# GpSimd splits weight slabs in quarters, and the mLSTM head loop is software-pipelined by one head

## The reference

```python
proj = xn @ w_in                                   # 1024 -> 4096
xm, z = jnp.split(proj, 2, axis=-1)                # 4 heads of 512 each
xp = jnp.concatenate([conv_state, xm], axis=1)
xc = conv_b + sum(xp[:, j:j + L] * conv_w[j] for j in range(4))
xc = jax.nn.silu(xc)
q = jnp.einsum('blhd,hde->blhe', xc_by_head, wq)   # and k
v = jnp.einsum('blhd,hde->blhe', xm_by_head, wv)
gates = concat(q, k, v) @ w_gates + b_gates
...
o = jax.nn.sigmoid(z)
```

## Time and profile before

| | before |
|---|---|
| median of three runs | 2535.7 us |
| profiled execution, its own time | 2533.09 us |
| its span | 2531.3 us |
| PE busy | 2311.2 us, 91% |
| PEld busy | 2138.8 us, 84% |
| DVE busy | 1268.1 us, 50% |
| POOL busy | 981.8 us, 39% |
| ACT busy | 340.9 us, 13% |
| mean granted clock of PE | 0.939 |
| chain of waits, by engine | PE 81%, DVE 15%, issue 2%, ACT 2% |

### The profile page before, as it was taken

How to read it: one execution, slowest core, us unless ns; L and a number is a source line. 1 busy time by engine, 2 the same in 40 slices (tenths; PEclk the granted TensorE clock), 3 DMA queues, 4 the chain that set the end, 5 groups by cost and what they waited for, 6 DMA issues and landing times.

```text
span 2531.3 us, 37962 instructions
## 1 busy us (share of the span) xinstructions
PE 2311.2 (91%) x16133; PEld 2138.8 (84%) x16133; DVE 1268.1 (50%) x2092; ACT 340.9 (13%) x578; POOL 981.8 (39%) x309
## 2 busy tenths in 40 slices
PE   7968758899999999989899889999979999999997
PEld 7967657897999999989898766577659889999997
DVE  7765687633635254662653623443444436263354
ACT  4211211212200000120110121220212211000001
POOL 4524553532455555544444420012014244555552
PEclk9988888999999999999999888889889999999998
DMA  5112332310222222224324122241122112222221
GB/s 198 68 67 84 112 105 97 135 66 34 80 78 80 81 83 83 95 93 152 142 103 160 66 72 89 111 160 67 71 86 98 50 51 84 80 78 79 81 83 54
DMA packets 36593, 231.26 MB, mean 91 GB/s; under 512 B 4332, under 2 KB 7404, under 8 KB 10864
## 3 DMA queue, kind: packets, MB, share of 16 engines
q1 hardware_dynamic: 21600, 154.15, 17.2%
q10 hardware_dynamic: 14864, 75.21, 7.6%
HBM read 195.50 MB, written 33.85 MB: 91 GB/s over the span
## 4 chain that ended last, share of the span: by engine, by line
PE 81%; DVE 15%; issue 2%; ACT 2%; DMA 0%; ACTq 0%; DVEq 0%
PE psum L504 63%; PE psum L534 14%; PE psum L520 2%; DVE xnl L1403 2%; DVE xc L1952 1%; DVE bbq L1627 1%; PE psum L530 1%; DVE tm L1603 0%; DVE tm L2124 0%; DVE tm L2123 0%; DVE xnl L2126 0%; DVE x L1774 0%; DVE x L1536 0%; ACT pr L1189 0%; DVE xc L1950 0%
## 5 line engine op out<-in xcount | busy, mean ns | idle before, releaser
L454 POOL TENSOR_SCALAR whi<-raw 128x2048 fp32r<-128x2048 f32 x146 | 289.2, 1981 | 1494.7 <-PE psum L504 1426.4
L504 PE MATMUL psum<-xnh,whi 128*128 128x288 f32 (+1 forms) x2816 | 630.2, 302 | 79.2 <-DVE xnl L1403 30.3
L456 POOL TENSOR_TENSOR wlo<-raw,whi 128x2048 fp32r<-128x2048 f32 x146 | 682.9, 4678 | 12.2
L504 PE MATMUL psum<-xnl,whi 128*128 128x288 f32 (+1 forms) x2816 | 622.9, 300 | 0.0
L504 PE MATMUL psum<-xnh,wlo 128*128 128x288 f32 (+1 forms) x2816 | 622.3, 299 | 0.0
L504 PEld LDWEIGHTS psum<-xnh,whi 128*128 128x128 f32 x2816 | 469.2, 193 | 90.5 <-issue 55.3
L504 PEld LDWEIGHTS psum<-xnl,whi 128*128 128x128 f32 x2816 | 469.1, 193 | 0.0
L504 PEld LDWEIGHTS psum<-xnh,wlo 128*128 128x128 f32 x2816 | 468.9, 193 | 0.0
L504 PE MATMUL psum<-hh,whi 128*128 128x288 f32 x1024 | 220.1, 296 | 0.0
L504 PE MATMUL psum<-hl,whi 128*128 128x288 f32 x1024 | 219.4, 295 | 0.0
L504 PE MATMUL psum<-hh,wlo 128*128 128x288 f32 x1024 | 219.3, 295 | 0.0
(11 more groups left out here) (395 smaller groups left out, 2808.7 us busy)
## 6 DMA issues: line engine op xcount, KB each, us to landing
raw<-in_w SPq DMA_DIRECT2D x146, 1024.0 KB, 4.7
C<-in_C ACTq DMA_DIRECT2D x4, 1024.0 KB, 4.9
o_cp<-mvt ACTq DMA_DIRECT2D x4, 1024.0 KB, 3.9
o_cs<-C ACTq DMA_DIRECT2D x4, 1024.0 KB, 3.9
t_xc<-xc ACTq DMA_DIRECT2D x3, 1152.0 KB, 4.1
t_z<-mv ACTq DMA_DIRECT2D x3, 1152.0 KB, 4.4
t_q<-mq ACTq DMA_DIRECT2D x3, 1152.0 KB, 4.1
t_k<-mk ACTq DMA_DIRECT2D x3, 1152.0 KB, 4.2
```

The source lines that it names most:

```text
L454: pool.tensor_scalar(whi[:, s, :], raw[:, s, :], 1.0, 1.0, ALU.mult, ALU.mult).then_inc(S("slab_hi"), 1)
L456: pool.tensor_tensor(wlo[:, s, :], raw[:, s, :], whi[:, s, :].bitcast(F32), ALU.subtract)\
L504: ins = pe.matmul(bank(g, 2 * m + b)[:, 0:t1 - t0], W[wi][:, kk, m0 + m, :], r[:, kk, t0:t1], start=(at_first and wi == 0 and r is rh), st ...
```

## The change

Three things are changed. First, POOL's `split` works on quarters of 512 columns: four times a tensor_scalar and a tensor_tensor; PE is still told once per slab, after the last. Second, the order of slabs and groups in the mLSTM inputs: xm of the next head comes before q, k, v of this one, z of the next head behind the gate of this one. Third, DVE and ACT follow: DVE does convolution tiles 0 and 1 of the next head before it copies q out, and tiles 2 and 3 each ahead of a z evacuation. For the last head tile 2 stands between the k and v copies. In head 0, tiles 0 and 1 come between the two xm evacuations. ACT does SiLU before it rounds xm, and begins a head's inputs after the stores of the head before.

```diff
@@ schedule(), and the same order in PE's loop
-            for h in range(ML_H):
-                for part in ("xm", "z"):
-                    for i in range(2):
-                        if (h, part, i) != LATE_Z:
-                            s("ml", h, part, i)
-                            g("ml", h, part, i)
+            inputs(0, "xm")
+            inputs(0, "z")
+            for h in range(ML_H):
+                if h + 1 < ML_H:
+                    inputs(h + 1, "xm")
                 for part in ("q", "k", "v"):
                     s("ml", h, part)
                     g("ml", h, part, 0)
                     g("ml", h, part, 1)
                 g("gate", h)
+                if h + 1 < ML_H:
+                    inputs(h + 1, "z")
@@ POOL
-                pool.tensor_scalar(whi[:, s, :], raw[:, s, :], 1.0, 1.0, ALU.mult, ALU.mult).then_inc(S("slab_hi"), 1)
-                pool.wait_ge(S("slab_hi"), i * 2 + (s + 1))
-                pool.tensor_tensor(wlo[:, s, :], raw[:, s, :], whi[:, s, :].bitcast(F32), ALU.subtract)\
-                    .then_inc(S("slab_split"), 1)
+                for piece in range(4):
+                    c = slice(SLAB // 4 * piece, SLAB // 4 * (piece + 1))
+                    pool.tensor_scalar(whi[:, s, c], raw[:, s, c], 1.0, 1.0, ALU.mult, ALU.mult).then_inc(S("slab_hi"), 1)
+                    pool.wait_ge(S("slab_hi"), i * 8 + (4 * s + piece + 1))
+                    ins = pool.tensor_tensor(wlo[:, s, c], raw[:, s, c], whi[:, s, c].bitcast(F32), ALU.subtract)
+                ins.then_inc(S("slab_split"), 1)
@@ ACT
+            head_inputs(0)
+            for h in range(ML_H):
                 if h < ML_H - 1:
                     for w, (nm_, buf) in enumerate((("q", mq), ("k", mk), ("v", mv))):
                         act.wait_ge(S("qkv_ready"), 6 * h + 2 * w + 2)
                         store(A["t_" + nm_][h], buf[:], nm_ + "_spilled")
+                    head_inputs(h + 1)
@@ DVE
+            def conv_inputs(h, i):
+                if h and i == 0:
+                    v.wait_ge(S("xm_hi"), h)
+                    v.wait_ge(S("xm_split"), h)
...
+            def conv(h, t):
+                if h and t == 0:
                     v.wait_ge(S("xc_spilled"), 16 * h)
...
+            for i in range(2):
+                conv_inputs(0, i)
+                conv(0, 2 * i)
+                conv(0, 2 * i + 1)
+            for t in range(ML_T):
+                low_xc(0, t)
+            scale_z(0, 0)
+            low_xm(0)
+            scale_z(0, 1)
+            for h in range(ML_H):
+                nxt = h + 1 < ML_H
+                if nxt:
+                    conv_inputs(h + 1, 0)
+                    conv(h + 1, 0)
+                    conv_inputs(h + 1, 1)
+                    conv(h + 1, 1)
                 for w, (part, buf) in enumerate((("q", mq), ("k", mk), ("v", mv))):
...
+                        if h + 1 == LATE_Z[0] and w == 1 and i == 1:
+                            conv(h + 1, 2)
+                    if nxt and w == 2:
+                        low_xc(h + 1, 0)
+                        low_xc(h + 1, 1)
                 g = GR["gate", h]
...
+                if nxt and h + 1 != LATE_Z[0]:
+                    conv(h + 1, 2)
+                    scale_z(h + 1, 0)
+                    conv(h + 1, 3)
+                    scale_z(h + 1, 1)
+                elif nxt:
+                    conv(h + 1, 3)
+                    scale_z(h + 1, 0)
+                if nxt:
+                    low_xc(h + 1, 2)
+                    low_xc(h + 1, 3)
+                    low_xm(h + 1)
```

More of the change, by code:

```diff
@@ L804, in _, with inputs @@
             mlp(0)
-            for h in range(ML_H):
[L806 to L811, removed]
+            def inputs(h, part):
+                for i in range(2):
+                    if (h, part, i) == (0, "xm", 0):
+                        project_first(3, GR["ml", h, part, i], SL["ml", h, part, i])
+                    elif (h, part, i) != LATE_Z:
+                        project(GR["ml", h, part, i], SL["ml", h, part, i], xnh, xnl)
+            inputs(0, "xm")
+            inputs(0, "z")
+            for h in range(ML_H):
+                if h + 1 < ML_H:
+                    inputs(h + 1, "xm")
                 for w, part in enumerate(("q", "k", "v")):
@@ L1912, in _ @@
             v.memset(xm[:, :, 0:3], 0.0)
[L1913 to L1938, removed]
@@ new lines, in conv_inputs @@
+            def conv_inputs(h, i):
+                if h and i == 0:
+                    v.wait_ge(S("xm_hi"), h)
+                    v.wait_ge(S("xm_split"), h)
+                g = GR["ml", h, "xm", i]
+                group_ready(v, g)
+                for m in range(2):
+                    for b, w, c0, c1, t0 in SEG:
+                        ins = tt(xm[:, 2 * i + m, c1:c1 + w], bank(g, 2 * m + b)[:, c0:c0 + w], rs[:, t0:t0 + w], MUL)
+                ch.mark(ins, free[g % 2], S("xm_ready"))
+                a = PCOL["conv_cache"][0] + 12 * h + 6 * i
+                cc = par[:, a:a + 6].rearrange("p (t k) -> p t k", k=3)
+                two, out = slice(2 * i, 2 * i + 2), slice(4 * h + 2 * i, 4 * h + 2 * i + 2)
+                ch.mark(v.tensor_copy(xm[:, two, TP + 3:TP + 6], cc))
+                v.tensor_copy(cst[:, 0, out, :], xm[:, two, TP:TP + 3])
+                v.tensor_copy(cst[:, 1, out, :], xm[:, two, T + 3:T + 6])
@@ L1958, in _ @@
-                low_xc(ML_T - 1)
-                if h:
-                    v.wait_ge(S("v_spilled"), 16 * h)
-                scale_z(0)
+                for tap in range(4):
+                    for d0, s0, w in ((0, 0, TP), (TP, TP + 3, TS)):
+                        src, dst = xm[:, t, s0 + tap:s0 + tap + w], xc[:, t, d0:d0 + w]
+                        wc = col("conv_w", 16 * h + 4 * t + tap)
+                        if tap == 0:
+                            ins = ts(dst, src, wc, col("conv_b", 4 * h + t), MUL, ADD)
+                        else:
+                            ins = stt(dst, src, wc, dst, MUL, ADD)
+                        ch.mark(ins)
+                    ch.sync()
@@ new lines, in conv, with low_xc, scale_z @@
+                v.sem_inc(S("conv_done"), 1)
+            def low_xc(h, t):
+                v.wait_ge(S("xc_hi"), 4 * h + t + 1)
+                tt(xcl[:, t, :], xc[:, t, :], xch[:, t, :].bitcast(F32), SUB).then_inc(S("xc_split"), 1)
+            def scale_z(h, i):
+                g = GR["ml", h, "z", i]
+                group_ready(v, g)
+                if h and i == 0:
+                    v.wait_ge(S("v_spilled"), 16 * h)
+                for b in range(4):
+                    dst = sz if (h, "z", i) == LATE_Z else mv
+                    ins = tt(halves(dst, 2 * i + b // 2)[b % 2], bank(g, b)[:, 0:HALF], RS[b % 2], MUL)
+                ch.mark(ins, free[g % 2], S("z_scaled"))
@@ L1962, in _, with low_xm @@
+            def low_xm(h):
                 v.wait_ge(S("xm_hi"), h + 1)
```

46 lines of the change are left out of this document (19 added, 27 removed).

## The result

The changed kernel takes 2463.9 us (median of 4 runs, 2461.6 to 2467.0) against 2536.5 us: ratio 0.972, 95% interval 0.970 to 0.973. It gains 72.6 us, where 35 were forecast; 2464 lies 13 us under the low end of the range. Its profiled execution has a span of 2460.2 us (2461.9 us of time), 71.1 less than before. Two executions, one of the kernel before (2913 us) and one of the changed kernel (5610 us), were slow ones and are left out of every comparison and median here.

A forecast was written before the change was run, and what follows sets the result against it. PE was taken as the bound, busy 91% of the span with 81% of the chain of waits. Terms 38.0 + 10 + 2 - 7 - 6 - 3 = 34.0 us gave 2499.1, plus 2.6 for the median: 2501 us, range 2486 to 2514.

The forecast's parts named there:

- The stage, 38.0: mLSTM inputs: projecting the next head's inputs ahead removes PE's holes before q; gain 38.0 us, bounds 33 and 43.
- the 5.9 us: mLSTM inputs: part of the 43.9 us excess that stays: 2.5 + 1.7 head 0, 0.8 heads 1 to 3, 0.9 head 3.
- The norm starts, +10: Starts of the four projections behind a norm: DVE's xnl tiles no longer held 4.3 us; +2.5 us each, +10 us.
- MLP hidden tile 3, -7: Last hidden tile of each MLP quarter, eight times: POOL's later end delays PE; -7 us, bounds 0 and -13.
- 720.6 becomes 721.5: MLP: POOL ends 1.2 us later, only DVE's casts slip in between, so PE's tile starts later by these times.
- POOL late in the MLP: Rival: hand-overs make each of 64 MLP slabs 0.85 us late, 54 us; time 2552 us; chance 0.05.
- S5, -6: S5's dense DVE rows delay slab splitting: -3.5 net including a smaller GLU stall, -2.5 for bbq products; bounds +6 and -12.
- a dense row of them now gives way eight times per slab: DVE rows without pause: quarters make them yield to POOL eight times per slab instead of twice, charged as a loss.
- The first 160 us, -3: Start of the kernel, chains of 0.2 us DVE instructions: -0.5 to -1 us per slab over four slabs, -3 us.
- Lone stalls, +2: Smaller stalls of lone DVE instructions on the chain: +2 us.
- clean gain: Rival: 15 DVE holds outside the stage each shrink by 3.1 us, 46 us; 2452 us; 0.13 for it or half.
- the 1 us wait before hidden tile 3: Sign of being right: in each MLP quarter PE waits about 1 us before hidden tile 3.

## Why the prediction was wrong

Direction, mechanism of the stage, and most signs were right; the size was half. By its own terms:

- **The stage, 38.0.** Measured 44.8, above the upper bound of 43; of the 5.9 us only 0.6 stayed, and the least time for the stage, 346.3 us, was itself 1.4 us too long. Head 0 was to keep 2.5 us and 1.7 of slow clock: 0.6 stayed and no clock loss. The 0.8 us for q's banks in heads 1 to 3 and the 0.9 in head 3 are absent. With whole slabs the sum would have been right by luck (39.0, holes of 2.7 and 3.2). The step that was mis-sized is POOL's share in these rows. Convolution tile 1 was given 3.7 us of its own and 5.3 of POOL's pieces, to end 11.3 us behind the start T of q; head 2's takes 7.30 us, 3.6 of them POOL's, and ends at T+10.45:

```profile
1226.62 1.74 DVE L1962 TENSOR_SCALAR xc<-xm,par 128x512 f32<-128x512 f32 x2
1228.39 5.53 DVE L1964 SCALAR_TENSOR_TENSOR xc<-xm,par,xc 128x512 f32<-128x512 f32 x6
```

- **The norm starts, +10.** Measured 16.3: 4.8 and 4.8 at the cross attentions, 3.2 and 3.5 at the MLPs (first matmul to the last of the norm's sums, 17.6 to 14.3 and 19.1 to 15.5 us). At a cross attention PE's waits there fall from 5.0 to 1.8 us, the whole hole of 3.2, and the matmuls give 1.6 more; the forecast had 2.8, less 1.0 for late sums, and 0.7 of clock. The late sums do not come. The six tiles answer to the earlier trace rows:

```profile
487.74 7.82 DVE L1425 SCALAR_TENSOR_TENSOR xnl<-x,par,xnh 128x576 fp32r<-128x576 f32 x6 [0.24 <-DVE x L1796]
```

1.3 us a tile, under the 1.6 us that PE takes, and never a tile 4 us late.
- **MLP hidden tile 3, -7.** Measured -2.3 for both MLPs (411.3 to 412.4 and 397.5 to 398.7 us). The step "720.6 becomes 721.5", so that PE is 0.9 us late, fails: I let the four subtractions wait for POOL's end, as in the earlier trace rows, but with pieces they slip in between.

```profile
695.60 3.46 DVE L1895 CAST hh<-hs 128x288 fp32r<-128x288 f32 x4
699.09 2.95 DVE L1899 TENSOR_TENSOR hl<-hs,hh 128x288 fp32r<-128x288 f32 x4
```

```profile
702.09 0.54 PE L513 MATMUL psum<-hh,whi 128*128 128x288 f32 x2 [0.21 <-DVE hl L1899]
```

PE waits 0.2 us, and in all four quarters of the first MLP 0.8 us. The rival "POOL late in the MLP" is wrong even with eighths.
- **S5, -6.** Measured +9.7 for attention and GLU. The slab's end did come late, and PE's wait for it grew from 3.0 to 9.9 us, as forecast; but the DVE row in front of it ended 4.6 us earlier, counted from the same block of PE, and PE's 288 matmuls behind that row took 11.38 us instead of 13.66. So the stretch from that block (324.45 before, 319.49 after) to PE's start behind slab 25 takes 80.3 us for 80.2: nothing instead of -3.5. The 2.9 us are won ahead of it (1.5 are lost from 269.10 to 296.21 of before, 4.4 won around them), where I had -2.5. And the GLU stall, which I let shrink only a little inside the net, is worth 5.5: 3.8 of wait and 1.7 of clock behind it. The other 1.3 of the GLU's 6.8 us are slow matmuls behind slab 25, 8.65 us before and 7.36 after. The sentence that failed is "a dense row of them now gives way eight times per slab": true as a count, false as a price (5.9, 5.8 and 5.6 us per slab, above): turns were charged that cost nothing, and the 4.8 us that the row ahead of slab 25 gains by meeting fewer pieces were not seen.
- **The first 160 us, -3.** Measured +2.0; the same sentence again. The forecast had named this sign itself: an end of the first 460 us earlier than now "would say that dense rows gain too". Per slab they break even; lone instructions among them gain.
- **Lone stalls, +2.** Measured 3.3 (1.8 in the cells, 1.5 in the output projections).
- **Not in the sum:** the clock of the cross attentions, -2.3 here by chance.

The sum was off in two small places as well. A whole slab made 1.2 us dearer by quarters was right: undisturbed pairs start 1.96 us apart in the changed kernel, four take 7.8 us, and the 8.4 us of the longer distance would have made the 1.2 a half larger, not a quarter. And 2535.7 less 34.0 is 2501.7.

Together 44.8 + 16.3 - 2.3 + 9.7 + 2.0 + 3.3 - 2.3 = 71.5, against a span 71.1 shorter (0.3 of the rest is the final norm, which takes longer). The rival "clean gain" came nearest by its time, 2452, at a chance of 0.13 with its half, but its arithmetic of 46 us outside the stage is not what happened: 28.6. Of the signs listed, those on POOL's counts hold, its means are a little above the forecast's, 0.72 and 1.38 us; one is wrong with its step, the 1 us wait before hidden tile 3, and the stage ends 44.8 us earlier, not 36 to 40. No DVE instruction is stretched by more than 1.1 us, as listed (it was 4.4 us).

Shown by runs: the shares of order and quarters, the price of a dense row, head 0's part, the place of the z evacuations. Only argued: that the 4.8 us which need both edits are the holds inside convolution tiles (cutting either of POOL's two instructions alone brings the stage to 44.8 or 43.9 us). Each MLP is 1.1 to 1.2 us longer; the waits before hidden tile 3 are 0.8 of that in the first, and the rest was not followed up.

## What to carry to other kernels

Where two engines lock each other out, a dense row pays about the same for the other's work however finely that is cut (5.9 us here for a slab of 6.6), and an instruction that stands alone on the path pays one piece at most; cutting finer is nearly free for the first and a gain for the second. What it costs is the time of the engine that is cut, in rows where the other's instructions are long (8.7, 15.3, 18.2 us a slab): there the slab with a waiting reader is better left whole. And price a hole with its clock: the GLU's, shortened by 3.8 us to under a microsecond, gave back 5.5.

## What the runs showed of the hardware that was not expected

The split's instructions have a fixed part. A tensor_scalar of 512 and 2048 columns takes 0.62 and 1.92 us, a tensor_tensor 1.28 and 4.60; with 256 columns they take 0.41 and 0.72. Means in the whole run with eighths are 0.47 and 0.81 us, turns included.

The same program at the same place finds two clocks. In the second cross attention PE starts after 4.5 us of waiting for the softmax; the two windows are of the changed kernel's first and second profiled execution:

```profile
1959.26:1969.00 9.74, 9.74 (x55) 8.30 (x56) 0.69 (x1) 2.66 (x5) 0.00 (x0) 0.82 0.01 2
```

```profile
1957.27:1967.00 9.73, 9.73 (x46) 9.73 (x47) 0.00 (x0) 2.06 (x4) 0.00 (x0) 0.50 0.01 2
```

One has 0.82, the other the lower level of 1.2 GHz throughout, and the 448 matmuls there take 65.2 or 69.6 us. At the first cross attention these two executions agree, 66.1 us in both. Over the profiled runs both values occur at both cross attentions, in any pairing, so kernels some 4 us apart cannot be told apart by one execution.
